# Value products from raw x times the norm weight, in a hybrid attention and gated-MLP block on one Trainium2 core

## Chip, cores and metric

One core of one Trainium2 chip runs the whole program. The metric is the device time of one execution in microseconds (us), lower is better. TensorE is also called PE, VectorE DVE, ScalarE ACT, GpSimd POOL, and SyncE, which issues nearly all DMAs, SP.

## What is computed

One residual layer over x, 512 tokens by 1024 channels, float32. Cut to what matters:

```
h = x * rsqrt(mean(x*x, axis=-1) + 1e-6) * g            # RMSNorm, g: norm_mix_g
z = h @ w_in + b_in                                     # 1024 -> gates, FoX q,k,v,f, conv, NSA q,k,v,gates
y_a = fox_attention(q, k, v, f) @ w_br_a                # 8 heads, forget gate bias from log_sigmoid(f), cumsum
y_b = (cb * causal_dwconv(cc * cx, sc_conv_w)) @ w_br_b
y_c = nsa_attention(...) @ w_br_c                       # compressed, selected, window branches
x = x + (sigmoid(ga)*y_a + sigmoid(gb)*y_b + sigmoid(gc)*y_c) @ w_o
u, v = split(rmsnorm(x, norm_ffn_g) @ w_up);  x = x + (silu(causal_dwconv(u)) * v) @ w_down
out = rmsnorm(x, norm_final_g)
```

The norm's factor, 1/rms, is one number per token, and g is one number per input channel. So a projection of x*g, with each token's output row multiplied by that token's 1/rms before the bias is added, is the same projection of h.

## The kernel before

Each product of float32 matrices is made of three TensorE products: both operands are split into a high part (rounded to TensorE's float32r) and a low part (the rest), and high x high, high x low and low x high are summed in a bank (mm3, L685). So every weight piece is loaded by SP into one of two slots of `raw`, ScalarE copies it to `w_hi` (split_hi, L980), GpSimd subtracts that copy to make `w_lo` (split_lo, L586), and the counts `hi_split` and `lo_split` say how far each is. SP may reload a slot when GpSimd is done with it (raw_free), and ScalarE may overwrite `w_hi` when TensorE is done with its piece (`tile_done`). The activations are split in the same way into `h_hi` and `h_lo`, by ScalarE and VectorE.

The order on every engine is written out by hand. All of the change lies in the first 55 us:

- SP loads x in four quarters of 128 tokens (L418), then twelve small loads of biases and column constants into `rows1` and `rows2` (L424 to L432), weights 1 of the small value projection (L439), bias rows, weights 2, and the value pieces (load_v, L433). ScalarE's queue issues weights 0 (L1013).
- ScalarE sums the squares of each quarter (L1018) and takes the root. VectorE inverts it and writes the scaled quarter `x_n` (L1322). TensorE transposes `x_n` into eight banks of 128 channels by 512 tokens (x_tile, L782) and the constants into columns (L793).
- For each of the eight channel tiles k, ScalarE evicts `h_hi` = bank x g (L1025) and VectorE `h_lo` = bank x g - `h_hi` (L1329).
- The small value projection (values of the NSA selected and window branches, forget and gate logits, 288 columns) takes weight pieces 0, 1 and 2 with two, three and three channel tiles (L804): 24, 36 and 36 products. The FoX values (512 columns) take pieces 3 to 6 of two channel tiles each, 24 products a piece (L818). Tokens are the stationary side in both.
- VectorE evicts the small projection with its bias (L1337, L1338). From it come the gate: ScalarE copies the forget logits (L1040), VectorE and ScalarE alternate over `fe_step` (L1342, Exp L1044, Ln L1046, L1355, the scan L1358, L1360), with table loads on ScalarE.
- VectorE evicts the FoX values (L1364). Piece 7 is the first of the head projections (project, L697, called at L835), which read `h_hi` and `h_lo` as the moving side. All later work (attention pairs, mix, MLP) follows TensorE from there.

Value pieces 3 to 6 are called tiles 3 to 6 below. In the program's order ScalarE's split of piece 5 stands behind the tanh (L1042), that of piece 6 behind the Ln (L1047).

## Time and profile before

| | us |
|---|---|
| median of 3 runs | 912.33 |
| lowest and highest | 912.30, 912.53 |
| profiled execution | 912.69 |
| its span | 911.00 |
| busy TensorE, VectorE, ScalarE, GpSimd | 895.1, 505.0, 376.4, 384.4 |
| the chain that ended last | TensorE 94%, VectorE 2%, ScalarE, DMA and issue 1% each |

The span is the time from the first to the last instruction of one profiled execution. A chain row names what ran, from where the chain came to it. In a timeline row, the figure in brackets is the idle time of the engine before the instruction and what ended it. The start of a TensorE instruction is what counts in a packed row of products, since each lasts longer than the distance to the next.

### The profile page before, as it was taken

Reading aid. Unit: us, or ns where it says so; the run is one execution under the profiler, and the core shown is the slowest. Engines: PE = TensorE matmul, PEld = TensorE weight load, DVE = VectorE, ACT = ScalarE, POOL = GpSimd, SP = SyncE. Lnnn points to the kernel's source line nnn. Section 1 sums busy time; section 2 is a strip of 40 time slices with the busy share of each in tenths; the row PEclk is TensorE's granted clock in tenths of the full one; section 3 lists DMA queues with packets and bytes.
Section 4 is the critical chain, followed back from the end, with each engine's and each line's share of the span. In section 5 each row is a group of like instructions: output and inputs, shape, how many; then the busy total and the mean of one; then the engine's idle time right before and its main releaser. Section 6 shows DMA issues by size and latency. Waiting matters only on the chain.

```text
span 911.0 us, 13430 instructions
## 1 busy us (share of the span) xinstructions
PE 895.1 (98%) x4360; PEld 746.9 (82%) x4360; DVE 505.0 (55%) x971; ACT 376.4 (41%) x650; POOL 384.4 (42%) x201
## 2 busy tenths in 40 slices
PE   6999999999999999999999999999999999999997
PEld 5888888888888888888887787888888888888885
DVE  4335564658575755756657887666666666400004
ACT  6435364444544553454433444333333333311125
POOL 4454535443223333323234574444444444444441
PEclk9999999999999999999999999999999999999999
DMA  6344342422222322222247434444453333322232
GB/s 189 95 129 116 81 119 76 122 74 70 70 70 70 89 51 77 75 55 70 69 98 156 116 95 113 118 115 115 125 152 114 92 92 102 128 94 93 93 116 92
DMA packets 178930, 90.75 MB, mean 100 GB/s; under 512 B 54463, under 2 KB 169549, under 8 KB 178901
## 3 DMA queue, kind: packets, MB, share of 16 engines
q1 hardware_dynamic: 177813, 90.08, 35.6%
q10 hardware_dynamic: 1088, 0.30, 0.1%
q8 instruction: 17, 0.28, 0.1%
q14 instruction: 12, 0.10, 0.0%
HBM read 86.14 MB, written 4.21 MB: 99 GB/s over the span
## 4 chain that ended last, share of the span: by engine, by line
PE 94%; DVE 2%; ACT 1%; DMA 1%; issue 1%; POOL 0%; SPq 0%; ACTq 0%
PE z_bank L687 24%; PE z_bank L689 24%; PE z_bank L688 24%; PE s_bank L687 3%; PE s_bank L688 3%; PE s_bank L689 3%; PE s_bank L755 3%; PE s_bank L724 3%; PE s_bank L775 1%; PE s_bank L774 1%; PE o_bank L775 1%; PE o_bank L774 1%; DMA x_in<-in_x 1%; PE o_bank L689 1%; PE o_bank L688 1%
## 5 line engine op out<-in xcount | busy, mean ns | idle before, releaser
L588 POOL TENSOR_TENSOR w_lo<-raw,w_hi 128x1024 fp32r<-128x1024 f32 (+1 forms) x144 | 347.5, 2413 | 506.5 <-ACT w_hi L994 421.4
L687 PE MATMUL z_bank<-h_hi,w_hi 128*128 128x512 f32 x768 | 302.4, 394 | 0.1
L689 PE MATMUL z_bank<-h_hi,w_lo 128*128 128x512 f32 x768 | 299.2, 390 | 0.0
L688 PE MATMUL z_bank<-h_lo,w_hi 128*128 128x512 f32 x768 | 299.0, 389 | 0.0
L994 ACT ACTIVATE w_hi<-raw 128x1024 fp32r<-128x1024 f32 x116 | 122.3, 1054 | 171.6 <-PE z_bank L689 171.5
L687 PEld LDWEIGHTS z_bank<-h_hi,w_hi 128*128 128x128 f32 x768 | 144.2, 188 | 31.4 <-issue 0.8
L689 PEld LDWEIGHTS z_bank<-h_hi,w_lo 128*128 128x128 f32 x768 | 144.1, 188 | 30.4
L688 PEld LDWEIGHTS z_bank<-h_lo,w_hi 128*128 128x128 f32 x768 | 144.3, 188 | 29.0 <-issue 0.2
L1611 DVE SCALAR_TENSOR_TENSOR u_c<-u_t,cols,u_c 128x512 f32<-128x512 f32 x44 | 65.7, 1494 | 25.4 <-ACT u_c L1222 22.3
L1003 ACT ACTIVATE p_f<-p_f,neg_mx 128x128 f32<-128x128 f32 (+1 forms) x96 | 52.7, 551 | 44.4 <-DVE neg_mx L1474 28.9
L1626 DVE TENSOR_TENSOR y_out<-s_bank,x_t 128x512 f32<-128x512 f32 x5 | 3.4, 689 | 106.6 <-PE s_bank L689 106.6
L989 ACT ACTIVATE w_hi<-raw 128x1024 fp32r<-128x1024 f32 (+2 forms) x28 | 29.0, 1036 | 56.2 <-PE z_bank L689 38.6
L1620 DVE TENSOR_TENSOR act_lo<-u_c,act_hi 128x512 f32 x22 | 40.8, 1853 | 19.9 <-ACT act_hi L1230 19.9
L687 PE MATMUL z_bank<-br_hi,w_hi 128*128 128x512 f32 x128 | 50.1, 392 | 0.5 <-DVE br_lo L1580 0.3
L688 PE MATMUL z_bank<-br_lo,w_hi 128*128 128x512 f32 x128 | 49.8, 389 | 0.0
L689 PE MATMUL z_bank<-br_hi,w_lo 128*128 128x512 f32 x128 | 49.8, 389 | 0.0
L1226 ACT ACTIVATE u_c<-u_c 128x512 f32<-128x512 f32 x22 | 13.9, 633 | 71.9 <-DVE u_c L1611 71.9
L687 PE MATMUL s_bank<-w_hi,act_hi 128*128 128x512 f32 x105 | 40.8, 389 | 0.0
L688 PE MATMUL s_bank<-w_lo,act_hi 128*128 128x512 f32 x105 | 40.8, 389 | 0.0
L689 PE MATMUL s_bank<-w_hi,act_lo 128*128 128x512 f32 x105 | 40.8, 389 | 0.0
L1281 DVE TENSOR_TENSOR pt_lo<-s_bank,pt_hi 128x512 fp32r<-128x512 f32 x60 | 36.9, 678 | 3.4 <-PE s_bank L755 3.4
L1290 DVE CUSTOM_DVE_ANT_0 p_f<-s_bank,alibi 128x384 f32<-128x384 f32 (+2 forms) x64 | 27.2, 487 | 18.6 <-issue 18.5
(305 smaller groups left out, 1304.2 us busy)
## 6 DMA issues: line engine op xcount, KB each, us to landing
raw<-in_w_in SPq DMA_DIRECT2D x112, 256.0 KB, 3.2
raw<-in_w_up SPq DMA_DIRECT2D x88, 256.0 KB, 3.1
raw<-in_w_down SPq DMA_DIRECT2D x42, 256.0 KB, 2.9
raw<-in_w_o SPq DMA_DIRECT2D x16, 256.0 KB, 3.4
x_in<-in_x SPq DMA_DIRECT2D x4, 512.0 KB, 5.4
f_bias<-cum_scratch SPq DMA_DIRECT2D x4, 512.0 KB, 4.5
raw<-in_w_br_a SPq DMA_DIRECT2D x8, 256.0 KB, 3.0
raw<-in_w_br_b SPq DMA_DIRECT2D x8, 256.0 KB, 3.3
```

The lines of the kernel that those rows point to most:

```text
L588: pool.tensor_tensor(w_lo[:, slot, 0:wide], raw[:, slot, 0:wide], w_hi[:, slot, 0:wide].bitcast(F), ALU.subtract) \
L687: pe.matmul(out, w[0], r[0], start=first, stop=False)
L688: pe.matmul(out, w[0], r[1], start=False, stop=False)
L689: return pe.matmul(out, w[1], r[0], start=False, stop=last)
L724: mm = pe.matmul(S[bank][:, col:col + P_LEN[i]], (q_hi, q_hi, q_lo)[part][rows, toks], (kh, kl, kh)[part][rows, 0:P_LEN[i]], start=(part = ...
L755: mm = pe.transpose(S[bank][:, col + P128 * (i - j):col + P128 * (i - j + 1)], p_f[:, a, P_OFF[i] + P128 * j:P_OFF[i] + P128 * (j + 1)], i ...
L989: act.activation(w_hi[:, slot, 0:wide], raw[:, slot, 0:wide], ACT.Copy).then_inc(hi_split, 1)
L994: act.activation(w_hi[:, slot, :], raw[:, slot, :], ACT.Copy).then_inc(hi_split, 1)
L1003: act.activation(t, t, ACT.Exp, bias=neg_mx[:, a, i:i + 1], accum_out=p_sum[:, a, i:i + 1]).then_inc(exp_done, 1)
L1281: dve.tensor_tensor(dst, src, hi.bitcast(F), ALU.subtract).then_inc(pt_lo_done, 1)
L1611: dve.scalar_tensor_tensor(u_c[:, :], u_t[:, tap:SEQ + tap], cols2[:, ds(C_FFN + FT * tap + i, 1)], u_c[:, :], ALU.mult, ALU.add).then_inc ...
L1620: dve.tensor_tensor(act_lo[:, i, :], u_c[:, :], act_hi[:, i, :].bitcast(F), ALU.subtract).then_inc(act_lo_done, 1)
```

## The change

`x_n` is gone: TensorE transposes the raw quarters, and the banks times g are split into new tiles `xr_hi` and `xr_lo`, from which both value projections are made. Their evictions multiply by the token's factor `stat[:, 3]` and add the bias. The norm weight alone is loaded first (`rows_g`, on ScalarE's queue) and transposed. SP loads x and weights 0 to 2 first, in a new order with a wait for the third quarter ahead of weights 1; the small loads of constants come later, and their transposes stand ahead of tile 6. TensorE transposes the identity 16 times between the quarters (keep_clock). VectorE sums the last quarter's squares, and the root is taken for all four at once.

`h_hi` and `h_lo` are still needed by everything from piece 7 on. GpSimd adds `xr_hi` and `xr_lo` (add_parts, two ahead of each of its splits of pieces 3 to 6), SP stores the factors to memory and loads them back as a row on all partitions (`rs_row`), VectorE multiplies each tile by the row (scale_tile), ScalarE copies it to `h_hi` (scaled_hi) and VectorE subtracts (scaled_lo). TensorE waits for all eight before piece 7. ScalarE's split of piece 5 moves ahead of the gate.

```diff
+N_WARM = (6, 4, 0, 4, 2)
...
-            x_n = sb("x_n", [P128, QT, D_MODEL], F, s)
+            x_s = sb("x_s", [P128, KT, SEQ], F, s)
...
-            for t in range(QT):
+            def load_x(t):
                 sp.dma_start(x_in[:, t, :], x_v[:, t, :]).then_inc(x_loaded[t], 16)
-            def load_v2(n, logits):
-                load_v2_part(sp, n, logits)
+            def load_v2(n):
+                k0, k1 = V2_K[n]
+                to = raw[:, n % 2, 0:V2_W * (k1 - k0)].rearrange("p (k m) -> p k m", m=V2_W)
+                for c, o, m, done in ((0, O_VS, P128, raw_loaded[n % 2]), (P128, O_VW, P128, raw_loaded[n % 2]),
+                                      (V2_V, O_FF, FOX_HEADS, lg_loaded[n]), (V2_V + FOX_HEADS, O_NG, 3 * NSA_HEADS, lg_loaded[n])):
+                    sp.dma_start(to[:, :, c:c + m], w_k[:, k0:k1, o:o + m]).then_inc(done, 16)
+            load_x(0)
+            load_x(1)
+            load_v2(0)
+            load_x(2)
+            load_x(3)
+            sp.wait_ge(x_loaded[2], 16)
+            load_v2(1)
+            raw_free(2)
+            load_v2(2)
...
-            raw_free(2)
-            load_v2(2, False)
-            load_v2(2, True)
-            for n in range(N_V2, N_FOX):
+            load_v(N_V2)
+            sp.wait_ge(x_rs, 1)
+            sp.dma_start(rs_dram.rearrange("(p t) -> p t", t=QT), stat[:, 3, :]).then_inc(rs_stored, 16)
+            sp.wait_ge(rows_zero, 2)
+            for c, n, src in rows[0:2]:
+                sp.dma_start(rows1[c:c + n, :], src.rearrange("(r m) -> r m", m=P128)).then_inc(rows_loaded, 16)
+            sp.wait_ge(rs_stored, 16)
+            sp.dma_start(rs_row[:, :], rs_dram.rearrange("(a n) -> a n", a=1).to_broadcast([P128, SEQ])).then_inc(rs_loaded, 16)
+            load_v(N_V2 + 1)
+            for n in range(N_V2 + 2, N_FOX):
                 load_v(n)
...
+            def add_parts(k):
+                pool.wait_ge(xr_lo_done, k + 1)
+                pool.wait_ge(x_ss, QT - 1)
+                pool.wait_ge(last_ss, 1)
+                pool.tensor_tensor(x_s[:, k, :], xr_hi[:, k, :].bitcast(F), xr_lo[:, k, :].bitcast(F), ALU.add).then_inc(x_summed, 1)
             for n in range(N_V2):
                 split_lo_v2(n)
             for n in range(N_V2, N_FOX + 1):
+                if n < N_FOX:
+                    for k in range(2 * (n - N_V2), 2 * (n - N_V2) + 2):
+                        add_parts(k)
                 split_lo(n % 2, n)
...
+            def keep_clock(count):
+                for _ in range(count):
+                    pe.transpose(S[1][:, SEQ - P128:SEQ], ident[:, :], ident[:, :])
...
             pe.wait_ge(consts, 3)
-            for t in range(QT - 1):
-                pe.wait_ge(x_normed, t + 1)
-                for k in range(KT - 1):
-                    x_tile(k, t)
-            pe.wait_ge(rows_loaded, 16 * 12)
-            pe.transpose(Z[1][:, 0:N_COLS1], rows1[:, :], ident[0:N_COLS1, 0:N_COLS1])
-            for k in range(KT - 1):
-                if k % 4 == 0:
-                    pe.wait_ge(x_normed, QT + k // 4)
-                x_tile(k, QT - 1).then_inc(x_t, 1)
-            pe.wait_ge(cols_ready, 2)
+            keep_clock(N_WARM[0])
+            pe.wait_ge(gain_loaded, 16)
+            pe.transpose(Z[1][:, 0:KT], rows_g[:, :], ident[0:KT, 0:KT]).then_inc(gain_t, 1)
+            keep_clock(N_WARM[1])
             for t in range(QT):
-                mm = x_tile(KT - 1, t)
-            mm.then_inc(x_t, 1)
+                pe.wait_ge(x_loaded[t], 16)
+                for k in range(KT):
+                    if t == 0 and k == KT - 1:
+                        pe.wait_ge(gain_ready, 1)
+                    mm = x_tile(k, t)
+                    if t == QT - 1:
+                        mm.then_inc(x_t, 1)
+                if t < QT - 1:
+                    keep_clock(N_WARM[2 + t])
             for n, (k0, k1) in enumerate(V2_K):
                 pe.wait_ge(lo_split, n + 1)
-                for k in range(k0, k1):
-                    if k:
-                        pe.wait_ge(h_lo_done, max(k + 1, QT))
-                    o = V2_W * (k - k0)
-                    w = [p[:, n % 2, o:o + V2_W] for p in (w_hi, w_lo)]
-                    for t in range(QT):
-                        if k == 0:
-                            pe.wait_ge(h_lo_done, t + 1)
-                        toks = slice(P128 * t, P128 * t + P128)
-                        mm = mm3(v2_bank[t][:, 0:V2_W], (h_hi[:, k, toks], h_lo[:, k, toks]), w, k == 0, k == KT - 1)
+                for t in range(QT):
+                    toks = slice(P128 * t, P128 * t + P128)
+                    for k in range(k0, k1):
+                        if n == 0 or t == 0:
+                            pe.wait_ge(xr_lo_done, max(k, t) + 1)
+                        o = V2_W * (k - k0)
+                        w = [p[:, n % 2, o:o + V2_W] for p in (w_hi, w_lo)]
+                        mm = mm3(v2_bank[t][:, 0:V2_W], (xr_hi[:, k, toks], xr_lo[:, k, toks]), w, k == 0, k == KT - 1)
                 mm.then_inc(tile_done, 1)
...
             for n in range(N_V2, N_FOX):
+                if n == N_FOX - 1:
+                    pe.wait_ge(v2_ready, 3)
+                    pe.wait_ge(rows_loaded, 16 * 11)
+                    pe.transpose(O[:, 0:N_COLS1], rows1[:, :], ident[0:N_COLS1, 0:N_COLS1])
+                    pe.transpose(O[:, P128:P128 + N_COLS2], rows2[:, :], ident[0:N_COLS2, 0:N_COLS2]).then_inc(cols_t, 1)
...
+            pe.wait_ge(h_lo_done, KT)
             project(1, 0, N_FOX, Z_FOX[0])
...
-            for logits in (False, True):
+            act.dma_start(rows_g[:, :], norm_mix_g[0].rearrange("(r m) -> r m", m=P128)).then_inc(gain_loaded, 16)
...
-            for t in range(QT):
+            for t in range(QT - 1):
                 act.wait_ge(x_loaded[t], 16)
-                act.activation(x_n[:, t, :], x_in[:, t, :], ACT.Square, accum_out=stat[:, 0, t:t + 1]).then_inc(x_ss, 1)
-                act.wait_ge(x_ss, t + 1)
-                act.activation(stat[:, 2, t:t + 1], stat[:, 0, t:t + 1], ACT.Sqrt, bias=eps_c[:, :], scale=1.0 / D_MODEL).then_inc(x_sqrt, 1)
-            split_hi(0, 0, 0)
-            act.wait_ge(cols_ready, 2)
+                act.activation(x_s[:, 2 * t:2 * t + 2, :].rearrange("p k n -> p (k n)"), x_in[:, t, :], ACT.Square,
+                               accum_out=stat[:, 0, t:t + 1]).then_inc(x_ss, 1)
+                if t == 1:
+                    split_hi(0, 0, 0)
+            act.wait_ge(gain_ready, 1)
             for k in range(KT):
                 act.wait_ge(x_t, k + 1)
-                act.activation(h_hi[:, k, :], x_bank[k][:, :], ACT.Copy, scale=cols1[:, C_GMIX + k:C_GMIX + k + 1]).then_inc(h_hi_done, 1)
-                if k == 4:
+                act.activation(xr_hi[:, k, :], x_bank[k][:, :], ACT.Copy, scale=cols_g[:, k:k + 1]).then_inc(xr_hi_done, 1)
+                if k == 1:
                     split_hi(1, 1, 0)
-            split_hi(0, 2, 1)
+                elif k == 3:
+                    act.wait_ge(x_ss, QT - 1)
+                    act.wait_ge(last_ss, 1)
+                    act.activation(stat[:, 2, :], stat[:, 0, :], ACT.Sqrt, bias=eps_c[:, :], scale=1.0 / D_MODEL).then_inc(x_sqrt, 1)
+                elif k == 5:
+                    split_hi(0, 2, 1)
             split_hi(1, 3, 2)
             split_hi(0, 4, 3)
+            def scaled_hi(k):
+                act.wait_ge(x_scaled, k + 1)
+                act.activation(h_hi[:, k, :], x_s[:, k, :], ACT.Copy).then_inc(h_hi_done, 1)
...
+            split_hi(1, 5, 4)
             act.wait_ge(fg_t, 1)
             act.activation(fg[:, :], Z[1][0:FOX_HEADS, :], ACT.Copy).then_inc(z_free[1], 1)
             act.activation(lg_t[:, :, FOX_HEADS:], lg_t[:, :, FOX_HEADS:], ACT.Tanh, scale=0.5).then_inc(ng_tanh, 1)
-            split_hi(1, 5, 4)
             act.wait_ge(fe_step, 1)
             act.activation(fe[:, :], fe[:, :], ACT.Exp).then_inc(fe_step, 1)
             act.wait_ge(fe_step, 2)
             act.activation(fe[:, :], fe[:, :], ACT.Ln, bias=1.0).then_inc(fe_step, 1)
+            for k in range(4):
+                scaled_hi(k)
             split_hi(0, 6, 5)
+            for k in range(4, KT):
+                scaled_hi(k)
             split_hi(1, 7, 6)
+            act.wait_ge(cols_ready, 3)
             split_hi(0, 8, N_FOX)
...
-            for t in range(QT):
-                for p in range(parts):
-                    cols = slice(D_MODEL // parts * p, D_MODEL // parts * (p + 1))
-                    dve.tensor_scalar(x_n[:, t, cols], x_in[:, t, cols], stat[:, 3, t:t + 1], None, ALU.mult).then_inc(x_normed, 1)
-            dve.wait_ge(cols_t, 1)
-            dve.tensor_copy(cols1[:, :], Z[1][:, 0:N_COLS1]).then_inc(cols_ready, 1)
-            dve.tensor_copy(cols2[:, :], Z[1][:, P128:P128 + N_COLS2]).then_inc(cols_ready, 1)
+            dve.wait_ge(gain_t, 1)
+            dve.tensor_copy(cols_g[:, :], Z[1][:, 0:KT]).then_inc(gain_ready, 1)
...
+            t = QT - 1
+            dve.wait_ge(x_loaded[t], 16)
+            dve.tensor_tensor_reduce(x_s[:, 2 * t:2 * t + 2, :].rearrange("p k n -> p (k n)"), x_in[:, t, :], x_in[:, t, :],
+                                     1.0, 0.0, ALU.mult, ALU.add, stat[:, 0, t:t + 1]).then_inc(last_ss, 1)
+            dve.wait_ge(gain_ready, 1)
             for k in range(KT):
-                dve.wait_ge(h_hi_done, k + 1)
-                dve.scalar_tensor_tensor(h_lo[:, k, :], x_bank[k][:, :], cols1[:, C_GMIX + k:C_GMIX + k + 1],
-                                         h_hi[:, k, :].bitcast(F), ALU.mult, ALU.subtract).then_inc(h_lo_done, 1)
-            dve.wait_ge(cols_ready, 1)
-            dve.tensor_scalar(half_b[:, :], cols1[:, C_GATE:C_GATE + 24], 0.5, None, ALU.mult)
+                dve.wait_ge(xr_hi_done, k + 1)
+                dve.scalar_tensor_tensor(xr_lo[:, k, :], x_bank[k][:, :], cols_g[:, k:k + 1],
+                                         xr_hi[:, k, :].bitcast(F), ALU.mult, ALU.subtract).then_inc(xr_lo_done, 1)
+                if k == 4:
+                    dve.wait_ge(x_sqrt, 1)
+                    dve.reciprocal(stat[:, 3, :], stat[:, 2, :]).then_inc(x_rs, 1)
+            dve.wait_ge(x_rs, 1)
             dve.wait_ge(small_loaded, 16 * 5)
             dve.wait_ge(tile_done, N_V2)
             for t in (3, 0, 1, 2):
-                dve.tensor_tensor(lg_t[:, t, :], v2_bank[t][:, V2_V:V2_W], vb[:, BR_W + V2_V:BR_W + V2_W], ALU.add).then_inc(lg_ready, 1)
-                dve.tensor_tensor(v2_f[:, t, :, :].rearrange("p b d -> p (b d)"), v2_bank[t][:, 0:V2_V], vb[:, BR_W:BR_W + V2_V], ALU.add) \
-                    .then_inc(z_free[0] if t == 2 else v2_ready, 1)
+                dve.scalar_tensor_tensor(lg_t[:, t, :], v2_bank[t][:, V2_V:V2_W], stat[:, 3, t:t + 1],
+                                         vb[:, BR_W + V2_V:BR_W + V2_W], ALU.mult, ALU.add).then_inc(lg_ready, 1)
+                dve.scalar_tensor_tensor(v2_f[:, t, :, :].rearrange("p b d -> p (b d)"), v2_bank[t][:, 0:V2_V], stat[:, 3, t:t + 1],
+                                         vb[:, BR_W:BR_W + V2_V], ALU.mult, ALU.add).then_inc(z_free[0] if t == 2 else v2_ready, 1)
+            dve.wait_ge(rs_loaded, 16)
+            def scale_tile(k):
+                dve.wait_ge(x_summed, k + 1)
+                tile = x_s[:, k, :].rearrange("p (t q) -> p t q", t=QT)
+                dve.tensor_tensor(tile, tile, rs_row[:, :].rearrange("p (q t) -> p t q", t=QT), ALU.mult).then_inc(x_scaled, 1)
+            def scaled_lo(k):
+                dve.wait_ge(h_hi_done, k + 1)
+                dve.tensor_tensor(h_lo[:, k, :], x_s[:, k, :], h_hi[:, k, :].bitcast(F), ALU.subtract).then_inc(h_lo_done, 1)
+            for k in range(3):
+                scale_tile(k)
...
+            scale_tile(3)
+            for k in range(4, KT):
+                scale_tile(k)
+                scaled_lo(k - 4)
+            dve.wait_ge(cols_t, 1)
+            dve.tensor_copy(cols1[:, :], O[:, 0:N_COLS1]).then_inc(cols_ready, 1)
+            dve.tensor_copy(cols2[:, :], O[:, P128:P128 + N_COLS2]).then_inc(cols_ready, 1)
+            dve.wait_ge(cols_ready, 1)
+            dve.tensor_scalar(half_b[:, :], cols1[:, C_GATE:C_GATE + 24], 0.5, None, ALU.mult).then_inc(cols_ready, 1)
+            for k in range(4, KT):
+                scaled_lo(k)
             dve.wait_ge(tile_done, N_FOX)
             for t in range(QT):
-                dve.tensor_tensor(v_f[:, t, :], S[t][:, :], vb[:, 0:BR_W], ALU.add).then_inc(vf_ready, 1)
+                dve.scalar_tensor_tensor(v_f[:, t, :], S[t][:, :], stat[:, 3, t:t + 1], vb[:, 0:BR_W], ALU.mult, ALU.add).then_inc(vf_ready, 1)
```

Left out of the diff: new tiles and semaphores, the column numbers that shift since g has left `cols1`, load_v2_part, and the small loads, which are the same as before in their new place.

## Rows read from the trace of the kernel before

**Rows 1.** The page: chain that ended last, shares of the span by engine

```profile
PE 94%; DVE 2%; ACT 1%; DMA 1%; issue 1%; POOL 0%; SPq 0%; ACTq 0%
```

**Rows 2.** Chain that ended last, in order of time: start us, us, what

```profile
2.21 7.41 DMA x_in<-in_x
...
11.36 2.13 DVE x_n L1322 x2
...
38.79 2.40 POOL w_lo L588
...
41.23 0.50 PE s_bank L687
```

**Rows 3.** Stretches: busy PE, PEld, DVE, ACT, POOL; granted clock, DMA share, GB/s

```profile
2.00:9.60 7.60, 2.54 (x12) 2.47 (x13) 2.00 (x5) 5.71 (x11) 3.70 (x12) 1.00 1.01 336
7.00:12.15 5.15, 4.94 (x22) 4.47 (x23) 2.79 (x7) 3.88 (x10) 0.36 (x1) 1.00 1.02 253
15.48:29.48 14.00, 13.77 (x97) 12.91 (x98) 4.63 (x8) 5.92 (x9) 6.50 (x3) 1.00 0.34 88
29.48:52.25 22.77, 22.55 (x103) 18.25 (x102) 8.27 (x15) 9.81 (x12) 10.34 (x4) 1.00 0.40 116
```

**Rows 4.** Timeline of the start: start us, us, engine line op, tiles, form, count

```profile
7.72 1.27 PE L782 MATMUL s_bank<-ident,x_n 128*128 128x128 f32 x5
...
13.22 1.98 SPq L378 DMA_DIRECT2D raw<-in_w_in  x4
...
13.53 0.55 PE L782 MATMUL s_bank<-ident,x_n 128*128 128x128 f32 x3 [0.55 <-DVE x_n L1322]
...
13.86 0.69 ACT L1025 ACTIVATE h_hi<-s_bank,cols 128x512 fp32r<-128x512 f32 x1 [2.16 <-PE s_bank L782]
...
13.91 0.62 PE L782 MATMUL z_bank<-ident,x_n 128*128 128x128 f32 x4
...
14.58 0.75 DVE L1329 SCALAR_TENSOR_TENSOR h_lo<-s_bank,cols,h_hi 128x512 fp32r<-128x512 f32 x1 [0.76 <-ACT h_hi L1025]
...
15.48 0.37 PE L687 MATMUL s_bank<-w_hi,h_hi 128*128 128x288 f32 x1 [0.94 <-DVE h_lo L1329]
...
19.85 0.40 PE L687 MATMUL s_bank<-w_hi,h_hi 128*128 128x288 f32 x1 [0.23 <-POOL w_lo L588]
```

**Rows 5.** Half a microsecond of the start, columns as in rows 3

```profile
16.50:17.00 0.50, 0.50 (x4) 0.30 (x3) 0.50 (x2) 0.50 (x2) 0.00 (x0) 1.00 0.10 12
```

**Rows 6.** Lines of two inputs from SBUF: ns min/median/max, first and last start, form

```profile
L1367 DVE TENSOR_TENSOR fv_lo<-v_f,fv_hi x4: 678/679/964, 55.6 to 57.7; 128x512 fp32r<-128x512 f32 x4
...
L639 POOL TENSOR_TENSOR f_diag<-f_bias,tri x8: 1287/1301/1308, 61.9 to 180.2; 128x512 f32<-128x512 f32 x8
...
L1435 DVE TENSOR_TENSOR cz<-nk_hi,nk_lo x8: 615/626/2721, 214.6 to 221.8; 64x256 f32<-64x256 f32 x8
...
L1513 DVE TENSOR_TENSOR c_p<-c_p,c_mask x4: 409/410/411, 252.0 to 431.3; 128x256 f32<-128x256 f32 x4
...
L1620 DVE TENSOR_TENSOR act_lo<-u_c,act_hi x22: 693/1894/2189, 563.2 to 787.5; 128x512 f32 x22
```

**Rows 7.** Timeline, VectorE and GpSimd together, in two later stretches

```profile
601.47 2.44 POOL L588 TENSOR_TENSOR w_lo<-raw,w_hi 128x1024 fp32r<-128x1024 f32 x1 [3.14 <-ACT w_hi L994]
...
602.57 1.89 DVE L1620 TENSOR_TENSOR act_lo<-u_c,act_hi 128x512 f32 x1 [0.91 <-ACT act_hi L1230]
...
514.33 1.59 DVE L1593 SCALAR_TENSOR_TENSOR h_lo<-x,cols,h_hi 128x512 fp32r<-128x512 f32 x1 [1.23 <-ACT h_hi L1206]
...
515.33 1.75 POOL L674 TENSOR_TENSOR x_acc<-x_acc,x_sq 128x512 f32<-128x512 f32 x1
```

**Rows 8.** Timeline, VectorE and GpSimd around the scan of the gate

```profile
41.98 1.21 DVE L1358 TENSOR_TENSOR_SCAN fe<-f_one,fe 8x512 f32<-8x512 f32 x1
...
42.25 3.15 POOL L588 TENSOR_TENSOR w_lo<-raw,w_hi 128x1024 fp32r<-128x1024 f32 x1 [1.07 <-ACT w_hi L989]
...
43.23 2.44 DVE L1360 TENSOR_SCALAR fe<-fe 8x512 f32<-8x512 f32 x1
```

62 lines of the change are left out of this document (28 added, 34 removed).

## The prediction

> **What bounds the kernel now.** The page comes first: the chain that ended last lies on TensorE to 94% [rows 1]. So only TensorE's own holes can be won back, and the change touches one stretch, from the start to the first head projection at 52.25. The chain in order of time [rows 2] shows that stretch: the last quarter of x lands at 9.62, then follow its square sum, the scaling (2.13), transposes from 13.53, the high halves, and the first value product at 15.48. From there TensorE has few holes [rows 3]: 14.00 us hold 13.77 of work, the next 22.77 hold 22.55; in these 22.77 stand four value tiles of 24 products, 5.45 each, and 0.45 of small transposes. The largest later hole is before 41.23, behind GpSimd's 2.40 us split [rows 2]: 0.37 us. The profiled execution took 912.69 (span 911.00), 0.36 above the median of 912.33; the sum is made against 912.69 and 0.36 is taken off.
>
> **The start, what is removed.** Norm, scaling and the wait for the row transposes leave the way to the first product. What is left is copied from the same steps [rows 4]: transpose 13.53, high half 13.86, low half 14.58, product 15.48, so 1.95 in all and 0.90 from the low half's start. The order of loads on SP changes: weights 0 now stand between the quarters of x, and 12 row loads leave. From 2.0 to 9.6 the DMA engines were full, share 1.01 [rows 3], so the same bytes less the row loads put that at 9.1 (bounds 8.6 to 9.6) and the third quarter 1.3 earlier, at 7.8. VectorE squares the last quarter itself: 1024 columns with two inputs from SBUF, estimated at 1.2 from 0.68 for 512 [rows 6]; so the first low half starts at 10.45 and the first product at 11.35. Then a new wait bites: ScalarE splits weights 1 after two high halves, and SP may issue them only when the third quarter has landed. Such four loads took from 13.22 until the DMA engines emptied at 16.9, 3.7 us [rows 5]: landed at 11.5. Queued behind it are high halves 2 and up, so low half 3 starts at 13.75 instead of 12.4, and the first weight piece (24 products) ends at 15.55. The other 72 products take 9.63 (19.85 in [rows 4] to 29.48): the value tiles begin at 25.2, not 29.48. Gain 4.3; 3.4 if weights 1 land 1 us later, 4.6 at best. The warming transposes stand in waits and cost nothing.
>
> **The four value tiles.** Moving ScalarE's split of piece 5 ahead of its tanh and tables removes the 0.37 hole. The 128x112 and 128x98 transposes go ahead of tile 6, 0.3. With no new wait the first head projection would start at 25.2 + 4 x 5.45 + 0.45 + 0.3 = 47.75, 4.5 earlier than 52.25. The evictions with a factor cost what the sums cost. The DMAs are hidden: the row store and broadcast end about 22, before VectorE asks at 27 (five us of cover; beyond that each us delays scaling 0); piece loads wait for the same splits as before.
>
> **What the change adds.** Eight sums on GpSimd (1.30 each), eight scalings and eight subtractions on VectorE (0.68 each if contiguous) [rows 6], and eight copies on ScalarE (0.6, from 0.69 for such a tile out of a bank [rows 4]). All of VectorE's 16 and GpSimd's 8 read two tensors from SBUF. What that means when both run is in [rows 7]: the subtraction issued at 602.57 under a split that ends at 603.91 ends at 604.46, 1.89 instead of 0.68; it waits for GpSimd's whole instruction. At 514.33 the same, and then the sum queued behind the split takes 1.75 instead of 1.30: the engine that waits goes next. At 41.98 [rows 8] GpSimd waits for the scan (3.15 for 2.40), and then VectorE's tiny multiply for GpSimd (2.44). So the two take turns, each holding for its duration less about 0.14.
>
> The scaling reads the factor row with a step of four elements. Nearest row: 256 strided columns took 0.615 against 0.410 contiguous, so 512 take 0.68 + 0.4 = 1.08; I take that, with 0.68 as the lower end. The Trainium skill, "Vector Engine (DVE) Microarchitecture Reference", 5.2, gives 1.73 ns a column against 1.054 for one source that hops every element, hence an estimate of 1.04; its 2.50 for small steps would make it 1.4 and the sum some 2.5 worse.
>
> **Taking turns, in order of time** (steps from [rows 6, 8], with ScalarE's split at 1.05, GpSimd's at 2.40, 0.05 to 0.25 between engines; tile 3 starts at 25.2). VectorE's scalings 0 to 2 are ready at 27.1, but GpSimd splits piece 4 until 29.05 and then alternates with its sums 4 and 5: scaling 2 ends at 34.2. GpSimd takes the split of piece 5 (to 36.45, just before tile 5 needs it at 36.55). VectorE's first gate step, which waited there, ends at 37.0; two value subtractions alternate with sums 6 and 7 and end at 40.4. Only then come the gate's next step, scan and multiply (43.05; ScalarE's Ln, ready at 39.55, no longer sets this), and scaling 3 (44.15). **ScalarE has its split of piece 6 queued behind the copy of tile 3**: copy to 44.8, split to 45.8, GpSimd behind one more scaling to 49.15. Tile 6 starts at 49.2 against 42.3: stall 6.9. Then scalings 5 to 7 and subtractions 0 to 3, one of them held 2.15 by that split, end at 53.1; ScalarE splits piece 7 behind copy 7; GpSimd's splits of 7 and 8 each hold one more subtraction: the last of eight ends at 60.65. The head projection waits for all eight and starts at 60.7, 6.05 after tile 6 ends at 54.65. Sum: -4.5 + 6.9 + 6.05 = **+8.45**. Everything after is bound by TensorE and moves as a whole, since the eviction that used to start with it still does.
>
> A bound that needs no order: from 24.1 on GpSimd holds six sums x 1.16 + four splits x 2.26 = 16.0, VectorE 8 x 0.94 + 8 x 0.55 + 4 x 0.54 + 1.07 (scan) + 0.5 = 15.65. Packed without a gap that ends at 55.75; with contiguous scalings at 52.65. So even then nothing of the 4.5 is left.
>
> **Rivals.** (A) as above: 912.69 + 8.45 - 0.36 = 920.8; with scalings at 0.68 the same walk gives +5.3, 917.7. (B) A, and the clock falls in the two waits. After TensorE's first idle 7 us, five transposes took 1.27 from 7.72, 0.21 apart, and four took 0.62 from 13.91, 0.11 apart [rows 4]: one level against the other (1.2 and 2.4 GHz), though the granted clock reads 1.00 [rows 3]. The second restart is on the path: 0 to half of the 4.94 us of work up to 12.15 [rows 3], 2.5, so 923.3. No row shows a wait of 6 us in mid-kernel. The Trainium skill, "TensorE: Matmul & The Clock Gate", Part 1, has an idle array fall back to 1.2 GHz, which speaks for B. (C) **Faster**: the two engines do not take turns on these operands. Place: GpSimd's 1.30 us sums and VectorE's scalings after 27; price: the waits of the walk. Without them the gate steps follow ScalarE's Ln, and scaling 3, copy 3 and split 6 behind them make tile 6 only 1.5 to 1.9 late and the projection at most 0.75 more: 4.5 less these is 1.9 to 3.0 earlier than 52.25, so 910.0. It decides where the last subtraction ends before 50.5. For: the row with turns at short GpSimd instructions is one; against: the median of 22 subtractions of that line is 1.89 [rows 6]. (D) Gain and waits cancel, with scalings at 0.68 and hardly a gap: +0.4, 912.7. (E) The head start does not come, since weights 1 land late behind the last quarter and ScalarE stands before them: gain 2, 922.9.
>
> **How the numbers follow.** A 0.45, B 0.15, C 0.20, D 0.12, E 0.08. A change within 0.2% (1.8 us) can't be told from none; D lies there. So faster 0.20, same 0.12, slower 0.68. A's own range is 917.5 to 922. The whole range reaches from C's middle (910.0) to 924.5, B's time with weights 1 some 1.2 us late; below and above lie about 0.1 each. The time is A's, 920.8.
>
> **What would show it.** First value product near 11.4, second weight piece near 15.6, tile 3 near 25.2; VectorE's scalings after 27 lasting 2 us and more; TensorE idle ahead of tile 6 for GpSimd's split, and ahead of the first head projection for h_lo. I am wrong if the scalings last 1.1 or less beside GpSimd's sums, if the split of piece 6 starts before 40, or if the last subtraction ends before 50.

## Result and profile after

The changed kernel takes 921.63 us (median of 5 runs, 920.72 to 922.31) against 912.33 (912.13 to 912.70): ratio 1.0103, 95% interval 1.0092 to 1.0114, so 9.3 us slower. The profiled execution took 922.10, its span is 920.4 against 911.0.

The chain that ended last, shares by engine, on the page of the changed kernel (its row of before is in [rows 1]): TensorE has fallen from 94% to 92%, VectorE has gone from 2% to 4% and GpSimd from 0% to 1%.

```profile
PE 92%; DVE 4%; ACT 1%; issue 1%; DMA 1%; POOL 1%; SPq 0%; ACTq 0%; DVEq 0%
```

The same chain in order of time, changed kernel (start us, us, what), beside [rows 2]:

```profile
3.75 4.62 DMA x_in<-in_x
...
9.89 2.61 DMA raw<-in_w_in
...
13.41 0.68 ACT xr_hi L1061
14.12 0.76 DVE xr_lo L1374
14.92 0.40 PE z_bank L716
```

Stretches of the changed kernel, columns as in [rows 3]: the three value tiles 3 to 5 with the column transposes behind them, TensorE's wait, and tile 6.

```profile
26.17:43.43 17.26, 17.26 (x80) 13.84 (x78) 15.67 (x17) 9.43 (x13) 15.46 (x8) 1.00 0.33 97
43.43:53.52 10.09, 0.02 (x2) 0.00 (x1) 10.05 (x15) 4.93 (x7) 6.92 (x2) 0.60 0.00 1
53.52:61.74 8.22, 8.22 (x24) 6.52 (x25) 4.56 (x4) 0.00 (x0) 2.81 (x1) 0.66 0.59 161
```

Read downwards. Tile 3 starts at 26.17, not 29.48: 3.31 gained. To 43.43 TensorE has no hole at all. Then it does nothing for 10.07, while VectorE is busy for all of it, and tile 6 takes 8.22 where such a tile takes 5.45. The timeline of TensorE in the changed kernel shows where the 2.77 are: consecutive starts are 0.43 apart for 13 products, then 0.23. Granted clock 0.55, 0.50 and 0.58 in the three stretches of five us from 45 on, 1.00 ahead of them.

```profile
43.20 0.25 PE L854 MATMUL o_bank<-ident,rows 98*128 98x98 f32 x1
53.52 0.80 PE L716 MATMUL s_bank<-w_hi,xr_hi 128*128 128x512 f32 x1 [10.07 <-POOL w_lo L607]
54.11 0.63 PE L717 MATMUL s_bank<-w_lo,xr_hi 128*128 128x512 f32 x1
54.54 0.63 PE L718 MATMUL s_bank<-w_hi,xr_lo 128*128 128x512 f32 x1
...
58.81 0.56 PE L716 MATMUL s_bank<-w_hi,xr_hi 128*128 128x512 f32 x1
59.20 0.40 PE L717 MATMUL s_bank<-w_lo,xr_hi 128*128 128x512 f32 x1
59.44 0.40 PE L718 MATMUL s_bank<-w_hi,xr_lo 128*128 128x512 f32 x1
...
61.74 0.39 PE L716 MATMUL z_bank<-h_hi,w_hi 128*128 128x512 f32 x1
```

What TensorE waits for is GpSimd's subtraction of weight piece 6, 2.40 before [rows 2]. The timeline of the changed kernel from 46.4, VectorE and GpSimd:

```profile
46.44 1.06 DVE L1393 TENSOR_TENSOR x_s<-x_s,rs_row 128x512 f32<-128x512 f32 x1
46.60 6.87 POOL L607 TENSOR_TENSOR w_lo<-raw,w_hi 128x1024 fp32r<-128x1024 f32 x1 [4.96 <-ACT w_hi L1026]
47.43 0.67 DVE L1397 TENSOR_TENSOR h_lo<-x_s,h_hi 128x512 fp32r<-128x512 f32 x1
...
48.03 1.04 DVE L1393 TENSOR_TENSOR x_s<-x_s,rs_row 128x512 f32<-128x512 f32 x1
49.01 0.67 DVE L1397 TENSOR_TENSOR h_lo<-x_s,h_hi 128x512 fp32r<-128x512 f32 x1
...
51.18 0.25 DVE L1428 COPY cols<-o_bank 128x104 f32<-128x104 f32 x1
51.36 0.24 DVE L1429 COPY cols<-o_bank 128x98 f32<-128x98 f32 x1
51.52 1.98 DVE L1431 TENSOR_SCALAR half_b<-cols 128x24 f32<-128x24 f32 x1
```

The subtraction is issued at 46.60 and ends at 53.47, 2.3 after VectorE turns at 51.18 from operands in SBUF to a bank. VectorE's scalings (1.04 to 1.06) and subtractions (0.67) keep their times alone: GpSimd got no turn among them.

So the ledger of the first head projection, 61.74 against 52.25: -3.31 start, -0.37 for the hole ahead of tile 5 that closed, +0.32 for the column transposes ahead of tile 6, +10.07 wait, +2.77 slow products: +9.5. The rest of the program is the same: span less projection is 858.7 in both.

### The profile page after: what moved, and what is told of

Same layout as the page of the kernel before. It is cut to its first block, busy times and chain, and to the rows that moved or that the text cites. A ratio compares the mean times of both kernels' runs of the same rounds, so it can differ in the third digit from the quotient of the medians.

```text
span 920.4 us, 13499 instructions
## 1 busy us (share of the span) xinstructions
PE 899.7 (98%) x4377; PEld 751.2 (82%) x4377; DVE 523.5 (57%) x982; ACT 379.0 (41%) x653; POOL 402.6 (44%) x209
## 4 chain that ended last, share of the span: by engine, by line
PE 92%; DVE 4%; ACT 1%; issue 1%; DMA 1%; POOL 1%; SPq 0%; ACTq 0%; DVEq 0%
PE z_bank L716 24%; PE z_bank L718 23%; PE z_bank L717 23%; PE s_bank L716 3%; PE s_bank L717 3%; PE s_bank L718 3%; PE s_bank L784 3%; PE s_bank L753 3%; PE s_bank L804 1%; PE s_bank L803 1%; PE o_bank L804 1%; PE o_bank L803 1%; POOL w_lo L607 1%; DVE x_s L1393 1%; PE o_bank L717 1%
## 5 line engine op out<-in xcount | busy, mean ns | idle before, releaser
L607 POOL TENSOR_TENSOR w_lo<-raw,w_hi 128x1024 fp32r<-128x1024 f32 (+1 forms) x144 | 352.5, 2448 | 497.7 <-ACT w_hi L1031 421.4
```

Source lines behind the costliest of these rows:

```text
L607: pool.tensor_tensor(w_lo[:, slot, 0:wide], raw[:, slot, 0:wide], w_hi[:, slot, 0:wide].bitcast(F), ALU.subtract) \
```

## Experiments

Times are medians; "before" was run beside each (912.18 to 912.34). The columns of TensorE come from the profiled execution of each run.

```
run                 median   ratio to before [95%]      wait ahead of tile 6  projection
changed kernel      921.63   1.0103 [1.0092, 1.0114]    10.07                 61.74
e1_split_early      921.32   1.0100 [1.0085, 1.0116]    6.13                  60.47
e2_gaps             921.98   1.0106 [1.0090, 1.0121]    10.16                 61.44
e3_flat_row         920.71   1.0102 [1.0087, 1.0118]    5.3                   59.92
e4_warm             920.22   1.0086 [1.0073, 1.0100]    1.53 (80 transposes)  59.68
e5_let_in           919.15   1.0081 [1.0067, 1.0095]    6.91                  58.52
e6_let_in_early     920.75   1.0102 [1.0087, 1.0118]    2.2                   58.54
e7_no_h             912.09   1.0002 [0.9993, 1.0012]    1.89                  50.10
e8_banks            909.93   0.9980 [0.9971, 0.9989]    none                  49.34
e9_banks2           908.28   0.9959 [0.9945, 0.9972]    none                  47.61
e10_banks2_sbuf     909.44   0.9971 [0.9959, 0.9983]    none                  48.89
```

**e1, weight piece 6 earlier on ScalarE.**

```diff
-            for k in range(4):
+            for k in range(3):
                 scaled_hi(k)
             split_hi(0, 6, 5)
-            for k in range(4, KT):
+            for k in range(3, KT):
```

> ScalarE rounds weight piece 6 ahead of its fourth copy of h and not behind it, so that GpSimd can begin its subtraction near 43.5, ahead of VectorE's unbroken row of scalings and subtractions (43.9 to 51.2 in the changed kernel). Theory (GpSimd's subtraction is starved by that row: it gets in only where VectorE leaves the two-operand reads of SBUF): it starts before the row or right behind its first scaling, ends at 46 to 47.5, tile 6 starts there instead of at 53.5, the clock does not fall, and the projection waits for VectorE's last subtraction, at about 58.5: 918, between 917 and 919. Rival (the subtraction is slow for another reason, or lands in the row all the same): tile 6 starts at 51 or later and the time stays 921 to 922.

Measured 921.32: the rival's time, in its second form, since the subtraction lands in the row all the same. The timeline of GpSimd in e1, and of TensorE ahead of tile 5:

```profile
32.37 3.14 POOL L650 TENSOR_TENSOR x_s<-xr_hi,xr_lo 128x512 f32<-128x512 f32 x1
...
39.53 0.61 PE L716 MATMUL s_bank<-w_hi,xr_hi 128*128 128x512 f32 x1 [1.88 <-POOL w_lo L607]
...
43.28 9.83 POOL L607 TENSOR_TENSOR w_lo<-raw,w_hi 128x1024 fp32r<-128x1024 f32 x1
```

It was issued 3.3 earlier, behind its own sum, a quarter of a microsecond before the first scaling (43.53), and still ended at 53.1, 2.3 after VectorE's row ended at 50.83. It did not find VectorE free: the gate's last step, itself held by GpSimd's sum, ran until 43.60. The expectation that it would get in "before the row or right behind its first scaling" was wrong. TensorE's shorter wait (6.13) is no gain: in this execution piece 5 was late by 1.88, so that tile 5 itself started late and slow (8 products about 0.43 apart). That lateness says something too. It comes from the stretch ahead of e1's edit, where the program is that of the changed kernel: there GpSimd's sum of 32.11 got in behind one scaling and took 2.16; here the sum of 32.37 was passed over by the next scaling (33.28 to 34.35) and took 3.14, and piece 5 behind it came up against both value subtractions (4.01 for 3.24). So the order of the program alone does not decide whether the two take turns.

**e2, one-element writes between the instructions of the row.**

```diff
             for k in range(4, KT):
+                dve.memset(pad_small[:, 2 * k:2 * k + 1], 0.0)
                 scale_tile(k)
+                dve.memset(pad_small[:, 2 * k + 1:2 * k + 2], 0.0)
                 scaled_lo(k - 4)
```

> Order as in the changed kernel, but VectorE writes one element of an unused cell before each of the eight instructions of the row, so that two reads of two SBUF operands never stand back to back. Theory (starvation by instructions that follow each other directly): GpSimd's subtraction of piece 6, which comes ready near 46.6, gets in at the next such write and takes at most 2.5 to 4 us in place of 6.87, tile 6 starts at 49 to 50.5 in place of 53.5: 918 to 920. Rival (GpSimd only gets in where VectorE reads a bank, or where its row is over): nothing changes but eight small writes, 921.5 to 922.5.

Measured 921.98, GpSimd 6.95 for piece 6. VectorE's timeline in e2 shows that this was no gap. In the program the write L1427 stands between a scaling and the subtraction L1397. It begins at 45.27, when the scaling ahead of it (44.25 to 45.32) still runs and the subtraction behind it has already begun (45.26).

```profile
43.27 2.05 DVE L1393 TENSOR_TENSOR x_s<-x_s,rs_row 128x512 f32<-128x512 f32 x2
...
45.26 0.67 DVE L1397 TENSOR_TENSOR h_lo<-x_s,h_hi 128x512 fp32r<-128x512 f32 x1
45.27 0.06 DVE L1427 MEMSET pad_small<- 128x1 f32 x1
45.87 1.06 DVE L1393 TENSOR_TENSOR x_s<-x_s,rs_row 128x512 f32<-128x512 f32 x1
```

The run tells nothing against starvation; it only shows that a small write opens no gap.

**e3, the factor row in the order of h's tokens.**

```diff
-sp.dma_start(rs_dram.rearrange("(p t) -> p t", t=QT), stat[:, 3, :])
+sp.dma_start(rs_dram.rearrange("(t p) -> p t", t=QT), stat[:, 3, :])
-dve.tensor_tensor(tile, tile, rs_row[:, :].rearrange("p (q t) -> p t q", t=QT), ALU.mult)
+dve.tensor_tensor(x_s[:, k, :], x_s[:, k, :], rs_row[:, :], ALU.mult)
```

> The row of factors is stored in the order of the tokens of h, so a scaling reads it element by element and not every fourth; the store becomes 512 writes of 4 bytes. Nothing is left out. Theory (the stride costs 1.04 - 0.68 = 0.36 us in each scaling, and GpSimd waits for the end of the row): the row of four scalings and four subtractions shortens by 1.4 and the scaling before it by 0.4, GpSimd gets in at about 49.3 in place of 51.2, tile 6 at 51.6: 919.5 to 920. Rival A (the scaling does not depend on the stride): 921.6. Rival B (the 4-byte store lands after 28.7 and holds up the scalings): slower than 921.6.

Measured 920.71 (920.28 to 923.51, a wide spread; the ratio can't be told from that of the changed kernel). Both the theory's term and rival B's are in the trace. The scaling's line in e3 (ns min/median/max):

```profile
L1392 DVE TENSOR_TENSOR x_s<-x_s,rs_row x8: 671/673/692, 29.8 to 49.5; 128x512 f32<-128x512 f32 x8
...
  DMA rs_row<-rs_scratch: 1.2, 1
```

The stride costs 1.04 - 0.67 = 0.37 a scaling, as expected, while the store of 4-byte pieces took 9.2 to land and not 4.5, so VectorE started 1.2 late. It also held up SP, which waits for the store before it loads weight piece 4: that load was issued at 25.91 and not at 21.36. ScalarE's timeline in e3:

```profile
31.21 1.06 ACT L1026 ACTIVATE w_hi<-raw 128x1024 fp32r<-128x1024 f32 x1 [8.67 <-DMA raw<-in_w_in]
```

TensorE waited 2.67 for piece 4, and 5.3 for piece 6, which VectorE's row held as before (5.33 from 47.64).

**e4, TensorE kept busy through the wait.**

```diff
+                    pe.wait_ge(z_free[0], 1)
+                    for _ in range(80):
+                        pe.transpose(Z[0][:, SEQ - P128:SEQ], ident[:, :], ident[:, :])
```

> TensorE makes 80 transposes of the identity into a free bank behind the transposes of the rows, in the time in which it waits for weight piece 6; no other engine's work changes. They take 80 x 0.11 = 8.9 us of the wait of 10.07. Theory (tile 6 runs its first 13 products at 0.43 because TensorE had been idle): tile 6 still starts at 53.5 but takes 5.45 in place of 8.22, and VectorE's last subtraction (58.08) is ready before its end: 918.9, between 918.5 and 919.3. Rival (the slow products have another cause, as the operands' own reads): 921.6 as before.

TensorE's timeline in e4:

```profile
43.63 8.90 PE L857 MATMUL z_bank<-ident 128*128 128x128 f32 x80
...
54.06 0.50 PE L716 MATMUL s_bank<-w_hi,xr_hi 128*128 128x512 f32 x1 [1.53 <-POOL w_lo L607]
...
59.68 0.39 PE L716 MATMUL z_bank<-h_hi,w_hi 128*128 128x512 f32 x1
```

Tile 6 took 5.62, not 8.22, and the granted clock is 1.00 in every stretch: 2.6 of the loss is the clock's lower level (0.43 apart against 0.23, 1.2 against 2.4 GHz) after TensorE had stood idle, and work with no use of its own holds it off. The time fell by 1.4 only (1.9 between the profiled executions), 920.22, above the range expected: tile 6 began at 54.06, not 53.52. Of these 0.54, 0.3 come from the start, which moves from one execution to the next: here the last quarter of x landed at 9.95 and not 9.67, and the columns were transposed at 43.45 and not 43.11. The rest lies in VectorE's row, whose scalings took 1.08 to 1.11 here. The Trainium skill, "TensorE: Matmul & The Clock Gate", Part 1, has an idle array fall back to 1.2 GHz: the trace agrees, with 13 products 0.43 apart behind 10.07 of idle time and none behind the transposes.

**e5, VectorE waits for GpSimd inside the row.**

```diff
             for k in range(4, KT):
+                if k == 6:
+                    dve.wait_ge(lo_split, 7)
                 scale_tile(k)
```

> As the changed kernel, but VectorE waits in the middle of its row, ahead of the seventh scaling, until GpSimd's subtraction of weight piece 6 has ended. In the first runs eight one-element writes between the instructions of the row let GpSimd in nowhere (they ran beside the instruction ahead of them), and a subtraction that came at 43.3, ahead of the row, was held to its end too; what is left to show is that VectorE's row is what holds it. Theory (it is the row): the subtraction gets in at about 48.1, ends at 50.5, tile 6 starts there and not at 53.5, and the last subtraction of h, which the row's pause sets back, is at 57 to 59.5: projection at 58 to 59.5 in place of 61.7, 917.8 to 919.5. Rival (GpSimd itself is late): tile 6 at 53 or later, 921 to 922.

The timeline of e5:

```profile
46.27 3.70 POOL L607 TENSOR_TENSOR w_lo<-raw,w_hi 128x1024 fp32r<-128x1024 f32 x1 [4.97 <-ACT w_hi L1026]
47.09 0.67 DVE L1397 TENSOR_TENSOR h_lo<-x_s,h_hi 128x512 fp32r<-128x512 f32 x1
...
50.00 1.08 DVE L1393 TENSOR_TENSOR x_s<-x_s,rs_row 128x512 f32<-128x512 f32 x1 [2.24 <-POOL w_lo L607]
...
50.02 0.80 PE L716 MATMUL s_bank<-w_hi,xr_hi 128*128 128x512 f32 x1 [6.91 <-POOL w_lo L607]
```

GpSimd's piece 6 ends at 49.97, so its own 2.40 fill VectorE's pause, from 47.76 to 50.00. So it is VectorE's row that held it. 919.15, inside the range expected. Tile 6 starts 3.5 earlier than in the changed kernel and the projection 3.2, since it now waits 0.66 for piece 7; 0.3 to 0.4 of that is only an earlier landing of x in this execution. By the medians the gain is 2.5. Tile 6 is slow as before (11 products).

**e6, GpSimd let in ahead of the row.** e1's order, and `dve.wait_ge(lo_split, 7)` ahead of the fourth scaling.

> Piece 6 is rounded by ScalarE ahead of the fourth copy of h, and VectorE waits for GpSimd's subtraction of it before it starts the row at all. Tile 6 should start near 46, 2.6 after the tile before it, and end near 51.5 at the full clock. What is left is the sum of VectorE's work on h: five scalings, eight subtractions and the copies of the columns, 11.4 from 45.9, and up to 2.4 more behind GpSimd's piece 7. Theory (the second of the two stalls of the prediction returns as soon as the first goes, since VectorE has the work to do): TensorE waits 6 to 8 for the last subtraction, the projection starts at 57.3 to 59.7 and begins slow after that wait: 918 to 920.5. Rival (the whole loss hangs on piece 6 alone): projection near 51.5, 911 to 912.

Tile 6 waits 2.2 and runs at the full clock, but TensorE then stands idle ahead of the projection (waits of TensorE in e6, from 40 to 60):

```profile
PE z_bank L716 <- POOL w_lo L607: 7.0, 1, 7.0
PE s_bank L716 <- POOL w_lo L607: 2.2, 1, 2.2
```

920.75, 0.25 above the range expected. A second stall ahead of the projection comes as soon as the first goes, and the first products behind it are slow in turn (7 of them about 0.43 apart). One thing I had not expected: what ends it is not the last subtraction of h (56.2) but piece 7, which ScalarE rounds behind its last copy of h at 53.31 and GpSimd then needs 3.96 for, beside VectorE's subtractions (54.43 to 58.39). VectorE's work on h alone would account for 4.7 of the 7.0.

**e7, the work on h left out.** Sums gone; scalings and subtractions cut to 8 of 512 columns.

```diff
-                    for k in range(2 * (n - N_V2), 2 * (n - N_V2) + 2):
-                        add_parts(k)
-                dve.tensor_tensor(tile, tile, rs_row[:, :].rearrange("p (q t) -> p t q", t=QT), ALU.mult)
+                dve.tensor_tensor(x_s[:, k, 0:8], x_s[:, k, 0:8], rs_row[:, 0:8], ALU.mult)
```

> Leaves out the work on h: GpSimd's eight sums, and of VectorE's eight scalings and eight subtractions all but 8 of 512 columns; the low half of h is zeros written by GpSimd at the start. The values, their evictions and every product on TensorE stay. Theory (the head start of the changed kernel is worth 3.3 and all of the loss of 12.7 behind it comes from the work on h): tile 6 starts at 43.5 and the projection at 49: 908.5 to 909.5. Rival (part of the loss is the evictions and the new order of the queues): 911 or more.

The profiled execution has a span of 908.7 (910.47 in all) and the projection at 50.10. That is 11.6 earlier than in the changed kernel, which loses 12.7 behind its head start. It is 1 later than expected, since piece 6 still waited for its place in ScalarE's queue behind the fourth copy, which waits for the gate's steps on VectorE:

```profile
44.53 0.50 PE L715 MATMUL s_bank<-w_hi,xr_hi 128*128 128x512 f32 x1 [1.89 <-POOL w_lo L607]
```

But the median of its 11 runs is 912.09 (910.47 to 913.36), the rival's number, and the profiled run is the fastest of them. So the work on h is worth 9.5 by the medians and 11.6 by the one profile: most of the loss either way; that it is all of it is not shown. Why these runs spread is open. The evictions with a factor, which the rival names, stand in e8 and e9 too, and these are faster than the kernel before.

**e8, h made from the banks of x.** The main lines:

```diff
+                        dve.tensor_scalar(x_s[:, 6, P128 * t:P128 * t + P128], ones[:, :], stat[:, 3, t:t + 1], None, ALU.mult)
...
+                        mm = pe.transpose(Z[1][:, toks], x_s[:, 6, toks], ident[:, :])
...
+            act.activation(rs_row[:, :], Z[1][:, :], ACT.Copy)
...
+            for k in range(4, KT - 1):
+                dve.scalar_tensor_tensor(x_s[:, k, :], x_bank[k][:, :], cols_g[:, k:k + 1], rs_row[:, :], ALU.mult, ALU.mult)
...
+                dve.tensor_tensor(x_s[:, k, :], x_s[:, k, :], Z[1][:, :], ALU.mult)
...
+            dve.wait_ge(lo_split, 7)
```

The first line stands behind VectorE's reciprocal, the transposes behind weight piece 1, the three tiles from banks ahead of the evictions (tile 7 is copied from its bank and then scaled), the four scalings from the bank `Z[1]` behind them, the wait ahead of the last gate steps and two subtractions. ScalarE's copies of h move to where these tiles are ready. The store and load of the row are gone, and GpSimd adds tiles 0 to 3 only.

> The same change with the work on h arranged otherwise, nothing left out: TensorE spreads the norm's factors into a bank by four transposes and ScalarE copies them to SBUF, in place of the store and load through memory; VectorE makes four tiles of h straight from the banks of the raw x in the time in which it waits for the value tiles, and scales the four others from the bank; GpSimd adds four tiles and not eight; VectorE splits the last two tiles behind a wait for GpSimd's piece 6. By the rows of the changed kernel all of h is split by 45 and neither piece 5 nor piece 6 waits. Theory (the change loses only by where the work on h lies): tile 6 at 43.5 to 44, projection at 49 to 49.8, 908.7 to 910, under the kernel before. Rival (scalings that read a bank hold GpSimd as those that read SBUF do, or the early work holds up the value tiles): tile 4, 5 or 6 waits again, 911 to 916.

Measured 909.93, ratio 0.9980 (0.9971 to 0.9989): faster than the kernel before. Neither piece 4, 5 nor 6 is waited for (TensorE waits 0.34 for a scaling, between tiles 3 and 4), projection at 49.34. GpSimd and VectorE in e8 where they meet, timeline:

```profile
24.55 1.39 DVE L1401 TENSOR_TENSOR h_lo<-x_s,h_hi 128x512 fp32r<-128x512 f32 x1
25.34 1.76 POOL L646 TENSOR_TENSOR x_s<-xr_hi,xr_lo 128x512 f32<-128x512 f32 x1
...
27.05 1.74 POOL L646 TENSOR_TENSOR x_s<-xr_hi,xr_lo 128x512 f32<-128x512 f32 x1
28.75 2.41 POOL L603 TENSOR_TENSOR w_lo<-raw,w_hi 128x1024 fp32r<-128x1024 f32 x1
...
29.77 0.67 DVE L1421 TENSOR_TENSOR x_s<-x_s,z_bank 128x512 f32<-128x512 f32 x1
```

Two subtractions and two sums took turns and cost each other, and put the evictions off by 1.4; the scaling of 29.77 reads a bank and runs in 0.67 inside GpSimd's 2.41, both as if alone.

**e9, the same with two steps moved.**

```diff
-                if k == 1:
+                if k == 3:
                     split_hi(1, 1, 0)
...
-            scaled_lo(0)
-            scaled_lo(1)
...
+            scaled_lo(0)
+            scaled_lo(1)
```

The two subtractions leave their place ahead of the evictions and stand behind the subtractions of the first mixer's values.

> The arrangement of the run before (h made from the banks) with two steps moved, nothing left out: VectorE's first two subtractions of h go from ahead of the evictions of the small value tiles, which they held from 26.2 to 27.57 in that run, to behind the first mixer's values, and ScalarE rounds weight piece 1, for which it waits 1.2 at the start, behind its fourth copy of x and not behind its second. Theory (TensorE's waits left are the 0.44 behind the evictions and 0.3 for the factors' bank before 32.3, and 0.3 to 0.4 of the hole of 1.0 at 13.2): projection at 48.4 to 48.8 in place of 49.34, 909.0 to 909.5 in place of 909.93. Rival (the subtractions are as much in the way at their new place, or piece 1 comes late): 909.9 or more.

Measured 908.28, ratio 0.9959 (0.9945 to 0.9972), the fastest version found: 4.0 under the kernel before, and better than expected. Its waits of TensorE from 11 to the projection at 47.61 are one:

```profile
PE s_bank L712 <- DVE xr_lo L1381: 1.0, 1, 1.0
```

The hole of 1.0 ahead of 14.2, of which I had expected a third, closed whole: ScalarE's 1.2 of waiting for weights 1 had held back the copies of x queued behind it.

**e10, its four last scalings from SBUF.**

```diff
-                dve.tensor_tensor(x_s[:, k, :], x_s[:, k, :], Z[1][:, :], ALU.mult)
+                dve.tensor_tensor(x_s[:, k, :], x_s[:, k, :], rs_row[:, :], ALU.mult)
```

> As the run sent with it, but the four last scalings read the row of factors from its copy in SBUF and not from the bank; their size is the same 128x512. Theory (an instruction of VectorE with one operand in a bank does not contend with GpSimd's subtraction, one with both in SBUF does): the first of the four waits from 28.4 to about 30.3 for GpSimd's piece 4 and the four end at 33 in place of 31; TensorE's transposes behind tile 3 wait for them 0.7 to 1, piece 5 may be held as well: 909.9 to 910.9, 0.7 to 1.5 above the run sent with it. Rival (operands in banks are no different for contention): the same time within 0.3 as the run sent with it.

Measured 909.44 against 908.28 on the same chip: +1.2, in the range expected. The timeline of e10:

```profile
27.57 4.22 DVE L1418 TENSOR_TENSOR x_s<-x_s,rs_row 128x512 f32<-128x512 f32 x4
...
31.85 0.61 PE L872 MATMUL z_bank<-ident,lg_t 128*32 128x128 f32 x4 [1.10 <-DVE x_s L1418]
```

The four took 2.47 in e9. The first of them came while GpSimd split piece 4 (27.02 to 29.43) and took 2.42 for 0.68; the other three met nothing. Same sizes, same neighbours, one operand's place changed: where the operand lies decides whether VectorE and GpSimd contend. It is worth 1.2 of the 13.4 between e9 and the changed kernel; the rest is the other rearrangements, which no run takes apart.

## Why the prediction came out as it did

The time forecast was 920.8, the time measured 921.63, and the forecast ledger was +8.45 against +9.5. The sum held; its terms did not all, and that it came out within 0.8 is in good part luck: the first wait was 3.2 longer, slow products cost 2.8 that the sum had not, the start gained 1.0 less, and against these stands a second stall of 6.05 that did not come.

**The start.** Forecast 4.3, measured 3.31. The mechanism was right to the step, the wait of ScalarE for weights 1 too. Mis-sized was the landing of x: 9.67 and not 9.1, just outside the bound given (9.6), and weights 1 landed at 12.5, not 11.5. The first product came at 11.82, tile 3 at 26.17 for 25.2. VectorE and ScalarE in the changed kernel:

```profile
9.67 1.22 DVE L1369 CUSTOM_DVE_ANT_0 x_s<-x_in 128x1024 f32<-128x1024 f32 x1 [5.95 <-DMA x_in<-in_x]
...
12.58 0.93 ACT L1026 ACTIVATE w_hi<-raw 128x864 fp32r<-128x864 f32 x1 [1.20 <-DMA raw<-in_w_in]
```

Part of the error on x is the execution that was profiled: with the same loads x landed at 9.20 in e2, 9.26 in e5 and 9.95 in e4. Weights 1 were late in every run from e1 to e7: ScalarE began on them between 11.86 (e7) and 12.94 (e4).

**The costs of what was added.** Scaling 1.04 to 1.06 (forecast 1.08), subtraction 0.67, sum 1.30: as forecast. e3 confirms that the stride makes the difference. The estimate of 1.04 from the 1.73 ns of the Trainium skill, "Vector Engine (DVE) Microarchitecture Reference", 5.2, agrees. Its 2.50, which the prediction weighed for small steps, is measured there with both sources, or the destination alone, stepping; the scaling steps in one source, and no scaling alone took 1.4.

**Taking turns.** Up to 37.5 the walk holds, each step 1.0 late as the start was: scaling 2 ended at 35.2 (34.2), piece 5 at 37.47 (36.45). In the timeline of the changed kernel VectorE and GpSimd alternate there:

```profile
28.68 2.31 DVE L1393 TENSOR_TENSOR x_s<-x_s,rs_row 128x512 f32<-128x512 f32 x1
30.00 2.14 POOL L650 TENSOR_TENSOR x_s<-xr_hi,xr_lo 128x512 f32<-128x512 f32 x1
```

The step that failed is "So the two take turns, each holding for its duration less about 0.14", carried from rows in which one instruction met one to a row of nine, five scalings and four subtractions from 43.87 to 51.25. GpSimd's sum 6 (37.44, 2.95) already waited for both of the value subtractions behind each other, and its piece 6 (46.60) for the scaling that ran and the five instructions behind it, the whole rest of the row. "GpSimd behind one more scaling to 49.15" became 53.47: the first stall was 10.07, not 6.9. e5 and e6 show that the cause is the row and nothing in GpSimd: given a pause, the same subtraction is done 2.2 after the pause begins (e5), and takes 2.41 ahead of the row (e6). The rest of that step, ScalarE's piece 6 queued behind the copy of tile 3, was right: 46.52 for 45.8.

**The clock.** Forecast as rival B, at the second restart, 2.5. It came at the first, and cost 2.77 (2.6 by e4). Case A by itself would have given less: A's order of waits and B's clock together made the result. What no row could show before, rows show now: a wait of 10.07 in mid-kernel is followed by 13 products at the lower level, of 7.0 (e6) by 7, of 6.91 (e5) by 11, of 6.13 (e1) by 8. The length of the wait alone does not say it: 2.2 (e6) and 1.89 (e7) were followed by none, but 1.88 ahead of tile 5 in e1 by 8 (granted clock 0.68 from 40 to 45), and 2.67 ahead of tile 4 in e3 by 7, from the fourth product on.

**The second stall.** Forecast 6.05, measured none. VectorE, never held in the row, ended h at 58.08 and not 60.65, while the first stall and the slow tile put tile 6's end to 61.74. The mechanism is there all the same, but shows only where the first stall is gone: in e6 TensorE waits 7.0, 4.7 of it for VectorE's subtractions, as the prediction has it, and the rest for piece 7, which the sum did not have. This is also why taking 7.9 off the largest wait of the profile (e6) brings 0.9.

**The bound without an order** ("Packed without a gap that ends at 55.75") was meant to say that nothing of the gain could be left. For this set of operations with these operands no run contradicts it (the earliest end of h is 56.13, in e5). It is no bound on the change: e8 and e9 need four sums less, make four tiles of h from banks in time that VectorE had idle, and read the factor from a bank; then the head start stands: the projection is 2.9 and 4.6 earlier than before. Rival C, faster, was not it: VectorE and GpSimd do contend on these operands. They do so in e8 too (24.55 to 28.79), which is fast all the same, since its work on h lies where TensorE does not wait for it; e10, with the operands of the change in the last four scalings, gives back only 1.2.

## What to carry to other kernels

- Where VectorE and GpSimd both read two operands from SBUF, a long unbroken row on VectorE can be one block for GpSimd and not a series of turns. Put a wait for GpSimd's critical instruction into the row, or give VectorE an operand that lies in a bank; a bank read beside GpSimd cost neither anything here (e8, e9 against e10).
- Before moving work off TensorE's path, add up what both engines must do before the point where TensorE needs all of it. If that exceeds the cover, closing one wait only opens the next (e6).
- A wait of TensorE can cost more than its length: 13 slow products behind 10.07 cost 2.8 more, 7 behind 7.0 (e6) 1.5, and even a wait of 1.88 was followed by some (e1). Idle transposes buy that back, but less than removing the wait.
